# Decoder layer on eight cores: normalised token tiles transposed by DMA instead of TensorE, reciprocal roots by GpSimd's power

## The chip, the cores and the metric

One Trainium2 chip, its 8 cores, one batch element (2048 tokens) on each; nothing is exchanged between cores. The metric is the device time of the slowest core in microseconds, as the median of repeated runs.

## What is computed

```python
h = rmsnorm(x, g_mix_norm)                      # x: (2048, 1024) f32 per core
q|k|v|glu_in|gate_in = h @ w_in + b_in          # 512|128|128|1024|2048 columns
y_attn = sliding_window_attention(q, k, v, sinks) @ w_attn_proj   # window 128, 8 query and 2 key heads
z = a * sigmoid(b)                              # GLU of glu_in, 512 channels
y_conv = silu(layernorm(causal_depthwise_conv31(z))) @ w_conv_proj + b
x = x + (sigmoid(g_attn) * y_attn + sigmoid(g_conv) * y_conv) @ w_out
x = x + (silu(h2 @ w_gate) * (h2 @ w_up)) @ w_down,  h2 = rmsnorm(x, g_ffn_norm), inner width 2816
out = rmsnorm(x, g_final)
```

## The kernel before

Tokens lie in 16 tiles of 128 (`NTT`) and 4 groups of 512 (`NTG`). Matmuls take bf16 operands and contract over the partitions, so a projection needs the normalised tokens transposed: `hT` holds them as 8 blocks of 128 features by 2048 tokens. A tile gets there in four steps: `rms_sq` (ACT, sum of squares), `rms_rstd` (ACT, 1/sqrt as Ln and then Exp with scale -0.5), `rms_apply` (DVE, times root and gain, bf16, into one of four buffers `xn`), and `rms_T`: eight 128x128 transposes on PE into one PSUM bank (line 703, or 688 for the first four tiles) and a copy from there to `hT` by DVE or ACT.

The program has three stages.

- Mixer, the loop over groups: key, value and query products, attention in four blocks (`att_scores`, a mask by affine_select on POOL at line 793, `att_pv`, `att_T`), then per group four `glu_unit`s, whose output goes through a scratch tensor in device memory (`fill_zs`: one write and four shifted reads, in SP's queue). The depthwise conv of a group (`conv_unit`, line 863) and its LayerNorm (`ln_stats`, `ln_norm`, `ln_silu`) run during the next group. In `ln_stats` the variance's root is Ln and Exp on ACT over 128x512 (`stB`), and `ln_norm` multiplies by it on POOL. The tiles of group g+1 are normalised and transposed in group g. The stage ends with the conv of group 3.
- Merge and out: `merge_unit` for 8 column blocks by 4 groups, then `out_tile` for 16 tiles (16 matmuls each, the residual added by DVE), each followed by the second RMSNorm and `rms_T`. In program text tile t is transposed after the product of tile t+3 (`rms_T(tt - 3, "act")`); the last three are transposed inside the FFN, before its third group of tokens (`late_T`).
- FFN: in four passes over the 22 inner blocks, up products over the 4 groups of tokens, down products over the 16 tiles; the last pass has the final norm and the stores.

The order on each engine is not that of the text. A list scheduler (`Sched.schedule`) goes through all recorded operations with a cost for each (`ecost` for DVE and POOL, `DMA_RATE` in bytes per us and `DMA_LAT` for transfers), takes on every engine what can start first, and among those within a small slack the earliest in the text. It also deals out the PSUM banks: four for single tiles in the mixer (`ONE`), all eight from the merges of column block 2 on (`ANY`). So an altered cost or a removed operation moves others. Each engine then runs its list in order and waits on semaphores; that holds for the DMA issues in SP's and POOL's queues as well. Line 513 is every plain matmul, 517 every activation, 527, 533, 535 and 539 are the tensor-tensor and tensor-scalar helpers, 506 the DMA helper.

Of the kernel before, what the change touches and what calls it, by code (L numbers as in the profile page):

```python
# [11 lines left out]
ALU = mybir.AluOpType  # L12
# [5 lines left out]
NTG = 4  # L18
# [38 lines left out]
DMA_LAT = 2.0  # L57
DMA_RATE = 250e3
SLACK = {"pe": 0.05, "act": 0.25, "dve": 0.25, "pool": 0.3, "sp": 0.3}
# [9 lines left out]
class Sched:  # L69
# [80 lines left out]
    def schedule(self):  # L150
# [76 lines left out]
        while left:  # L227
# [28 lines left out]
            for op in blocks[k]:  # L256
                t += op.cost
                if op.dma:
                    q = e == "pool"
                    dma_free[q] = max(t, dma_free[q]) + op.nbytes / DMA_RATE  # L260
                    op.end = dma_free[q] + DMA_LAT
                else:
                    op.end = t
                order[e].append(op.gidx)
                for i in tiles_of.get(op, ()):
                    todo[i] -= 1
# [83 lines left out]
def record(plan):  # L350
# [49 lines left out]
    EPSB = region(32)  # L400
    EM = region(64)
    WCOL = region(16 * 8 * 4)
    DEN = region(16 * 4)
# [21 lines left out]
    rstd = A.f32(RSTDO, 48)  # L425
    epsb = A.f32(EPSB, 1)
    emask = A.bf16(EM, 32)
    wcol = A.f32(WCOL, 128).rearrange("p (g m) -> p g m", g=16)
# [93 lines left out]
    def ecost(eng, n, f=1.0):  # L522
        a, b = RATE[eng]
        return a + b * n * f
# [17 lines left out]
    def cp_(eng, out, in_, r, w):  # L542
        return S.add(eng, lambda e: e.tensor_copy(out=out, in_=in_), r, w, cost=ecost(eng, nfree(out)))

# [79 lines left out]
    op("pool", lambda e: e.memset(ss, 0.0), w=["ss"])  # L624
    op("pool", lambda e: e.memset(epsb, EPS), w=["epsb"])
    op("pool", lambda e: e.memset(onesf, 1.0), w=["onesf"])
    act(rstd[:, 0:1], epsb, AF.Ln, r=["epsb"], w=["warm"])
    op("pool", lambda e: e.iota(iota_i, [[1, 128]], base=0, channel_multiplier=-1), w=["iota"])
# [40 lines left out]
    def rms_rstd(c0, n):  # L669
        cs = ["ss%d" % c for c in range(c0, c0 + n)]  # L670
        rs = ["rstd%d" % c for c in range(c0, c0 + n)]
        act(rstd[:, c0:c0 + n], ss[:, c0:c0 + n], AF.Ln, r=cs + ["epsb", "warm"], w=rs, bias=epsb)
        act(rstd[:, c0:c0 + n], rstd[:, c0:c0 + n], AF.Exp, r=rs, w=rs, scale=-0.5)

# [6 lines left out]
    def rms_T(tt, copy_eng):  # L681
        b = tt % 4
        if copy_eng == "both":
# [15 lines left out]
            return  # L699
        bank = next_bank()  # L700
        S.begin()
        for c in range(8):
            op("pe", lambda e, c=c: e.transpose(out=ps_bf[bank.banks[0]][:, c * 128:(c + 1) * 128],  # L703
                                                in_=xn[:, b, c * 128:(c + 1) * 128], identity=ident),
               r=["xn%d" % b, "ident"], w=[bank], cost=0.075)
        S.end()
        src = ps_bf[bank.banks[0]].rearrange("p (c j) -> p c j", c=8)
        dst = hT[:, :, tt * 128:(tt + 1) * 128]
        if copy_eng == "act":
            act(dst, src, AF.Copy, r=[bank], w=["hT.%d" % tt])  # L710
        else:
            cp_(copy_eng, dst, src, r=[bank], w=["hT.%d" % tt])

# [159 lines left out]
    def ln_stats():  # L873
        bm = next_bank()
        S.begin()
        for c in range(4):
            mm(ps[bm.banks[0]], ones_bf, ybf[:, c, :], c == 0, c == 3, r=["ones", "ybf.%d" % c], w=[bm])
        S.end()
        bq = next_bank()
        S.begin()  # L880
        for c in range(4):
            mm(ps[bq.banks[0]], ones_bf, ysq[:, c, :], c == 0, c == 3, r=["ones", "ysq.%d" % c], w=[bq])
        S.end()
        act(stA, ps[bm.banks[0]], AF.Square, r=[bm], w=["stA"])
        tt_("dve", stB, ps[bq.banks[0]], stA, ALU.subtract, r=[bq, "stA"], w=["stB"])
        act(stB, stB, AF.Ln, r=["stB", "epsb"], w=["stB"], bias=epsb)
        act(stB, stB, AF.Exp, r=["stB"], w=["stB"], scale=-0.5)
        tt_("dve", stA, ps[bm.banks[0]], stB, ALU.mult, r=[bm, "stB"], w=["stA"])
# [39 lines left out]
    for tg in range(NTG):  # L928
# [40 lines left out]
        for u in range(4):  # L969
            glu_unit(tg, u)  # L970
            fill_zs(tg, u)
            if nxt < NTG:
                norm_apply(nxt, u)
                rms_T(4 * nxt + u, "dve")
            if prev >= 0:
# [102 lines left out]
    for tt in range(NTT):  # L1078
        out_tile(tt)
        if tt >= 1:  # L1080
            rms_apply(x2[tt - 1], tt - 1, 1, "x.%d" % (tt - 1))
        if tt >= 3:
            rms_T(tt - 3, "act")
    rms_apply(x2[NTT - 1], NTT - 1, 1, "x.%d" % (NTT - 1))

# [19 lines left out]
    S.alias(["wd0"], ["w_out0", "w_out1"])  # L1105
    late_T = [NTT - 3, NTT - 2, NTT - 1]
    f0 = 0
    si_ = 0
    for gi, nf in enumerate(FF_GROUPS):
# [4 lines left out]
        for fi in range(nf):  # L1114
            rg = w_next()
            ru = w_next()
            for tg in range(NTG):
                if late_T and tg == 2:
                    for tt in late_T:
                        rms_T(tt, "act")  # L1120
                    late_T = []
                    S.alias(["actT.%d.%d" % (f_, t_) for f_ in (4, 5) for t_ in range(NTG)],
                            ["xn%d" % i for i in range(4)])
                bg = proj_fm(tg, lambda k: ring[rg][:, k, :], ["ring%d.0" % rg, "ring%d.1" % rg])
# [76 lines left out]
```

How the kernel before makes its waits and increments, by code:

```python
            def body(eng):  # L302
                known = {}
                for op in self.ops[ename]:
                    waits = {}
                    for d in op.deps:
                        if d.dma:
                            key, val = ("d", d.eng, d.dsem), d.dticket
                        else:
                            key, val = ("c", d.eng), d.ticket
                        if known.get(key, 0) >= val:
                            continue
                        if waits.get(key, 0) < val:
                            waits[key] = val
                    for key, val in waits.items():
                        sem = csem[key[1]] if key[0] == "c" else dsem[key[1]][key[2]]
                        eng.wait_ge(sem, val)
                        known[key] = val
                    ins = op.fn(eng)
                    if ins is None:
                        continue
                    if op.dma:
                        ins.then_inc(dsem[ename][op.dsem], 16)
                    elif op.signal:
                        ins.then_inc(csem[ename], 1)
```

## Time and profile before

| | us |
|---|---|
| median of 3 runs (lowest, highest) | 922.11 (921.85, 923.03) |
| profiled execution | 923.55 |
| its span, first to last instruction, slowest core | 922.0 |
| spans of the eight cores | 912.3 to 922.0 |
| TensorE busy | 864.5 (94%) |
| VectorE, ScalarE, GpSimd busy | 401.1, 302.2, 211.7 |

The profile is of the slowest core. Busy shares count the time in which an engine executes an instruction; waits, register work and DMA issues are left out. Where TensorE is busy nearly always, the other engines matter by what they make it wait for.

### The profile page before, as it was taken

To read this page: it belongs to the slowest core of one execution; us is meant where nothing else is said; L and a number is where in the kernel's file an instruction comes from. 1 tells how busy PE (TensorE), PEld (TensorE's weight loads), DVE (VectorE), ACT (ScalarE), POOL (GpSimd) and SP (SyncE) were. 2 spreads that over 40 slices of the span, in tenths; PEclk is the share of its full clock that TensorE was granted. 3 is DMA by queue.
4 is the path that set the end of the run, shared out by engine and by line. 5 is a ranking of instruction groups with operands and counts; after the bars stand their busy time and mean duration, and the time that the engine had idled before them with its cause. 6 is when DMAs were issued, how large, how long until landed. Compare 5 with 4: busy or idle time off the path is not lost.

```text
span 922.0 us, 14159 instructions; the slowest of 8 cores (912.3 to 922.0 us)
## 1 busy us (share of the span) xinstructions
PE 864.5 (94%) x4837; PEld 405.0 (44%) x4923; DVE 401.1 (44%) x594; ACT 302.2 (33%) x490; POOL 211.7 (23%) x232
## 2 busy tenths in 40 slices
PE   4888798985999999999999999999999999999996
PEld 2344344432444444445544444444444444444442
DVE  3265677463554343456622263114512135212286
ACT  4183866463422222256631101110011100111186
POOL 3540717373542222210001101010001100000044
PEclk9898999999999999999999999999999999999998
DMA  9965222759975333390094404442064400000035
GB/s 178 150 152 176 66 78 66 100 91 140 189 117 54 35 35 35 35 226 15 13 148 47 37 10 71 44 46 24 3 89 46 39 8 1 1 1 1 1 160 206
DMA packets 102823, 67.64 MB, mean 73 GB/s; under 512 B 73875, under 2 KB 93505, under 8 KB 102753
## 3 DMA queue, kind: packets, MB, share of 16 engines
q0 software_dynamic: 83088, 29.37, 29.9%
q1 hardware_dynamic: 19248, 37.20, 13.5%
q8 instruction: 41, 0.67, 0.3%
q14 instruction: 29, 0.24, 0.1%
q10 hardware_dynamic: 417, 0.16, 0.1%
HBM read 85.56 MB, written 10.52 MB: 104 GB/s over the span
## 4 chain that ended last, share of the span: by engine, by line
PE 86%; DMA 8%; DVE 2%; ACT 2%; issue 2%; POOL 1%; SPq 0%; POOLq 0%; DVEq 0%; ACTq 0%
PE ps L513 82%; DMA arena<-w_in 4%; PE ps L863 2%; DMA z_scratch<-arena 2%; DMA arena<-z_scratch 1%; PE ps L703 1%; ACT arena L517 1%; DMA arena<-x 1%; POOL arena L506 1%; DVE arena L539 1%; ACT L517 0%; DVE arena L527 0%; PE ps L827 0%; SPq L506 0%; DVE arena L535 0%
## 5 line engine op out<-in xcount | busy, mean ns | idle before, releaser
L513 PE MATMUL ps<-arena 128*128 128x512 bf16 (+4 forms) x3940 | 811.2, 365 | 23.3 <-DMA arena<-w_in 7.0
L513 PEld LDWEIGHTS ps<-arena 128*128 128x128 bf16 (+1 forms) x4026 | 369.9, 99 | 454.2 <-issue 46.1
L527 DVE TENSOR_TENSOR arena<-arena,ps 128x512 f32<-128x512 f32 (+1 forms) x216 | 148.5, 687 | 292.3 <-PE ps L513 290.4
L517 ACT ACTIVATE arena<-ps 128x512 f32<-128x512 f32 (+3 forms) x159 | 113.3, 722 | 385.8 <-PE ps L513 363.1
L517 ACT ACTIVATE arena<-ps,arena 128x512 f32<-128x512 f32 (+1 forms) x112 | 75.4, 686 | 151.1 <-PE ps L513 107.8
L527 POOL TENSOR_TENSOR arena<-arena 128x512 f32<-128x512 f32 (+1 forms) x64 | 74.5, 1172 | 171.6 <-ACT arena L517 169.0
L517 ACT ACTIVATE arena<-arena 128x1 f32<-128x1 f32 (+3 forms) x152 | 91.6, 617 | 52.2 <-DVE arena L535 11.1
L539 DVE SCALAR_TENSOR_TENSOR arena<-ps,arena 128x512 f32<-128x512 f32 (+1 forms) x80 | 57.9, 725 | 95.7 <-PE ps L513 79.0
L506 POOL DMA_DIRECT2D arena<-w_ffn_in x44 | 38.7, 880 | 199.2 <-PE ps L513 199.2
L539 DVE SCALAR_TENSOR_TENSOR arena<-arena 128x1024 bf16<-128x1024 f32 (+2 forms) x64 | 68.1, 1064 | 14.4 <-ACT arena L517 12.5
L793 POOL TENSOR_SCALAR_AFFINE_SELECT arena<-arena 128x1024 bf16<-128x1024 bf16 x31 | 34.9, 1124 | 74.5 <-ACT arena L517 72.4
L863 PE MATMUL ps<-arena 128*32 128x512 bf16 x512 | 34.1, 415 | 11.5 <-DMA arena<-z_scratch 11.1
L535 POOL TENSOR_SCALAR arena<-arena 128x512 f32<-128x512 f32 x32 | 20.6, 644 | 88.0 <-ACT arena L517 87.8
L517 ACT ACT_TABLE_LOAD x19 | 24.4, 1283 | 26.0 <-PE ps L513 17.7
L527 DVE TENSOR_TENSOR arena<-ps,arena 128x512 bf16<-128x512 f32 (+2 forms) x44 | 21.8, 497 | 24.9 <-PE ps L513 15.2
L506 POOL DMA_DIRECT2D arena<-w_ffn_down x4 | 3.4, 842 | 126.1 <-PE ps L513 67.2
L539 DVE SCALAR_TENSOR_TENSOR arena<-arena,ps 128x512 f32<-128x512 f32 x32 | 21.8, 685 | 14.1 <-ACT arena L517 8.4
L863 PEld LDWEIGHTS ps<-arena 128*32 128x32 bf16 x512 | 13.9, 102 | 27.2 <-issue 18.0
L527 DVE TENSOR_TENSOR arena<-arena 128x512 bf16<-128x512 f32 (+1 forms) x35 | 22.7, 649 | 5.9 <-POOL arena L533 2.4
L506 POOL DMA_DIRECT2D arena<-w_in x23 | 20.8, 922 | 16.5 <-PE ps L513 10.7
L533 DVE TENSOR_SCALAR arena<-ps,arena 128x512 bf16<-128x512 f32 x20 | 14.9, 747 | 16.4 <-PE ps L513 14.4
L533 DVE TENSOR_SCALAR arena<-arena 128x512 f32<-128x512 f32 (+2 forms) x18 | 13.2, 736 | 19.7 <-ACT arena L517 19.6
(34 smaller groups left out, 126.0 us busy)
## 6 DMA issues: line engine op xcount, KB each, us to landing
arena<-x SPq DMA_DIRECT2D x32, 512.0 KB, 6.4
arena<-w_ffn_in POOLq DMA_DIRECT2D x44, 256.0 KB, 5.4
arena<-z_scratch SPq DMA_DIRECT2D x64, 135.0 KB, 3.1
out<-arena SPq DMA_DIRECT2D x16, 512.0 KB, 2.7
arena<-w_in POOLq DMA_DIRECT2D x16, 256.0 KB, 6.4
arena<-w_in POOLq DMA_DIRECT2D x7, 512.0 KB, 21.0
arena<-w_ffn_down POOLq DMA_DIRECT2D x2, 1536.0 KB, 13.1
arena<-w_ffn_down POOLq DMA_DIRECT2D x2, 1280.0 KB, 18.0
```

The lines of the kernel that those rows point to most:

```text
L506: return S.add(eng, lambda e: e.dma_start(out=out, in_=in_, **kw), r=r, w=w, dma=True, cost=0.95 if eng == "pool" else 0.45, nbytes=nb)
L513: return S.add("pe", lambda e: e.matmul(out=out, lhsT=lhsT, rhs=rhs, start=start, stop=stop, **kw), r, w, cost=max(0.06, nfree(rhs) * 0.00 ...
L517: return S.add("act", lambda e: e.activation(out=out, in_=in_, func=func, **kw), r, w, cost=0.22 + 0.00089 * nfree(in_))
L527: return S.add(eng, lambda e: e.tensor_tensor(out=out, in0=in0, in1=in1, op=alu), r, w, cost=ecost(eng, nfree(out)))
L533: return S.add(eng, lambda e: e.tensor_scalar(out=out, in0=in0, scalar1=s1, scalar2=None, op0=op0), r, w, cost=c)
L535: return S.add(eng, lambda e: e.tensor_scalar(out=out, in0=in0, scalar1=s1, scalar2=s2, op0=op0, op1=op1), r, w, cost=c)
L539: return S.add(eng, lambda e: e.scalar_tensor_tensor(out=out, in0=in0, scalar=scalar, in1=in1, op0=op0, op1=op1), r, w, cost=ecost(eng, nf ...
L703: op("pe", lambda e, c=c: e.transpose(out=ps_bf[bank.banks[0]][:, c * 128:(c + 1) * 128], in_=xn[:, b, c * 128:(c + 1) * 128], identity=id ...
L793: op("pool", lambda e, sl=sl, pat=pat, base=base, cm=cm: e.affine_select(out=sl, in_=sl, pattern=pat, base=base, channel_multiplier=cm, co ...
L863: op("pe", lambda e, m=m, cg=cg: e.matmul(out=ps[bank.banks[0]][32 * cg:32 * (cg + 1), :], lhsT=wS[:, 4 * c + cg, m, :], rhs=zs[c][:, cg, ...
```

## The change

The transposition of all tiles but the first four becomes one DMA each, from `xn` to `hT`, in SP's queue. The RMS roots and the LayerNorm root become an addition and a power of -0.5 on POOL (for LayerNorm the addition of eps goes into DVE's subtraction). The second norm's `rms_apply` and `rms_T` stand right behind their tile in the text, and there is no `late_T`. The scheduler's costs for copies and for transfer rates differ too.

```diff
-DMA_RATE = 250e3
+DMA_RATE = (370e3, 300e3)
...
+    mhalf = A.f32(MH, 8)
...
     def cp_(eng, out, in_, r, w):
-        return S.add(eng, lambda e: e.tensor_copy(out=out, in_=in_), r, w, cost=ecost(eng, nfree(out)))
+        return S.add(eng, lambda e: e.tensor_copy(out=out, in_=in_), r, w, cost=ecost(eng, nfree(out), 0.5 if eng == "dve" else 0.4))
...
+    op("pool", lambda e: e.memset(mhalf, -0.5), w=["mhalf"])
...
-    act(rstd[:, 0:1], epsb, AF.Ln, r=["epsb"], w=["warm"])
+    act(rstd[:, 0:1], epsb, AF.Exp, r=["epsb"], w=["rstd0"])
...
     def rms_rstd(c0, n):
         cs = ["ss%d" % c for c in range(c0, c0 + n)]
         rs = ["rstd%d" % c for c in range(c0, c0 + n)]
-        act(rstd[:, c0:c0 + n], ss[:, c0:c0 + n], AF.Ln, r=cs + ["epsb", "warm"], w=rs, bias=epsb)
-        act(rstd[:, c0:c0 + n], rstd[:, c0:c0 + n], AF.Exp, r=rs, w=rs, scale=-0.5)
+        ts_("pool", rstd[:, c0:c0 + n], ss[:, c0:c0 + n], EPS, None, ALU.add, None, r=cs, w=rs)
+        tt_("pool", rstd[:, c0:c0 + n], rstd[:, c0:c0 + n], mhalf[:, 0:n], ALU.pow, r=rs + ["mhalf"], w=rs)
...
-        bank = next_bank()
-        S.begin()
-        for c in range(8):
-            op("pe", lambda e, c=c: e.transpose(out=ps_bf[bank.banks[0]][:, c * 128:(c + 1) * 128],
-                                                in_=xn[:, b, c * 128:(c + 1) * 128], identity=ident),
-               r=["xn%d" % b, "ident"], w=[bank], cost=0.075)
-        S.end()
...
+        S.add("sp", lambda e: e.dma_start(out=hT[:, :, tt * 128:(tt + 1) * 128], in_=xn[:, b, :], transpose=True),
+              ["xn%d" % b], ["hT.%d" % tt], dma=True, cost=0.6, nbytes=262144)
...
-        tt_("dve", stB, ps[bq.banks[0]], stA, ALU.subtract, r=[bq, "stA"], w=["stB"])
-        act(stB, stB, AF.Ln, r=["stB", "epsb"], w=["stB"], bias=epsb)
-        act(stB, stB, AF.Exp, r=["stB"], w=["stB"], scale=-0.5)
+        stt_("dve", stB, ps[bq.banks[0]], EPS, stA, ALU.add, ALU.subtract, r=[bq, "stA"], w=["stB"])
+        tt_("pool", stB, stB, mhalf[:, 0:1].broadcast_to([128, 512]), ALU.pow, r=["stB", "mhalf"], w=["stB"])
...
     for tt in range(NTT):
         out_tile(tt)
-        if tt >= 1:
-            rms_apply(x2[tt - 1], tt - 1, 1, "x.%d" % (tt - 1))
-        if tt >= 3:
-            rms_T(tt - 3, "act")
-    rms_apply(x2[NTT - 1], NTT - 1, 1, "x.%d" % (NTT - 1))
+        rms_apply(x2[tt], tt, 1, "x.%d" % tt)
+        rms_T(tt, "dma")
```

The line numbers move: line 513 of before is 515 of the change, 527 is 529, 793 is 785, 827 is 819, 863 is 855, 506 is 508; the transposing DMA is line 703 of the change.

The order on PE at the end of the mixer. L863 (L855) are the conv's matmuls, 32 to a unit; between them stand merge products. Before:

```order
L827 MATMUL ps<-arena 128x128 x4
L863 MATMUL ps<-arena 32x512 x32
L513 MATMUL ps<-arena 128x512 x12
L863 MATMUL ps<-arena 32x512 x32
L513 MATMUL ps<-arena 128x512 x20
L863 MATMUL ps<-arena 32x512 x32
L513 MATMUL ps<-arena 128x512 x808
```

With the change:

```order
L819 MATMUL ps<-arena 128x128 x4
L855 MATMUL ps<-arena 32x512 x64
L515 MATMUL ps<-arena 128x512 x8
L855 MATMUL ps<-arena 32x512 x32
L515 MATMUL ps<-arena 128x512 x12
L855 MATMUL ps<-arena 32x512 x32
L515 MATMUL ps<-arena 128x512 x3124
```

The first two conv units now stand together, 8 and 12 matmuls lie between the next ones, and behind the last everything is one run without a transpose.

The order in SP's queue in group 0 with the change, from the transposition of tile 4 to that of tile 7 (z_scratch is the scratch tensor, x the tokens of later tiles); before, the same queue had only the scratch and x rows:

```order
L703 DMA_TRANSPOSE arena<-arena 128x8x128
L508 DMA z_scratch<-arena 128x512
L508 DMA arena<-x 128x1024
L508 DMA arena<-z_scratch 32x4x540 x4
L703 DMA_TRANSPOSE arena<-arena 128x8x128
L508 DMA arena<-z_scratch 32x4x540 x4
L508 DMA arena<-x 128x1024
L508 DMA z_scratch<-arena 128x512
L703 DMA_TRANSPOSE arena<-arena 128x8x128
```

Each transposition takes its turn behind scratch reads, which themselves wait for the scratch write before them.

The order in POOL's queue with the change around the first LayerNorm (L785 is the attention's mask; the third row, which waits for DVE alone, is the power, and the 128x512 rows behind it are the norm's products):

```order
L529 TENSOR_TENSOR arena<-arena 128x4 [waits c_pool]
L785 AFFINE_SELECT arena<-arena 128x1024 [waits c_act] x2
L529 TENSOR_TENSOR arena<-arena 128x512 [waits c_dve]
L785 AFFINE_SELECT arena<-arena 128x1024 [waits c_act]
L529 TENSOR_TENSOR arena<-arena 128x512 [waits c_pool]
L529 TENSOR_TENSOR arena<-arena 128x512 [waits c_dve,c_pool]
L785 AFFINE_SELECT arena<-arena 128x1024 [waits c_act]
L529 TENSOR_TENSOR arena<-arena 128x512
```

The power stands between two masks, and the masks behind it wait their turn in the same queue.

## Rows read from the trace of the kernel before

**Rows 1.** The page: busy time of the engines
```profile
PE 864.5 (94%) x4837; PEld 405.0 (44%) x4923; DVE 401.1 (44%) x594; ACT 302.2 (33%) x490; POOL 211.7 (23%) x232
```

**Rows 2.** Windows: start:end, us, busy time per engine, PE clock, DMA share, GB/s
```profile
0.00:60.00 60.00, 41.27 (x280) 21.56 (x285) 22.00 (x38) 26.53 (x47) 26.92 (x44) 0.94 0.87 155
60.00:250.00 190.00, 163.38 (x1456) 79.13 (x1474) 111.14 (x169) 105.41 (x151) 89.64 (x80) 0.96 0.60 116
...
880.00:922.00 42.00, 32.98 (x151) 14.86 (x152) 30.20 (x57) 29.92 (x60) 19.56 (x16) 0.94 0.50 201
```

**Rows 3.** Waits of PE from 60 to 250 us: us in total, times, longest
```profile
PE ps L863 <- DMA arena<-z_scratch: 11.1, 3, 4.3
PE ps L827 <- DVE arena L527: 5.9, 5, 2.3
PE ps L513 <- ACT arena L517: 5.4, 5, 1.7
```

**Rows 4.** Groups by shape: count | busy us, mean ns | idle before, releasers
```profile
L703 PE MATMUL ps<-arena 128*128 128x128 bf16 x224 | 16.8, 219 | 0.5 <-DVE arena L539 0.4
...
L517 ACT ACTIVATE arena<-ps 128x1024 bf16<-128x1024 bf16 x16 | 16.2, 1024 | 15.3 <-PE ps L703 15.3
```

**Rows 5.** Timeline of PE in the out stage: start us, us, what
```profile
408.55 0.61 PE L703 MATMUL ps<-arena 128*128 128x128 bf16 x8
...
409.00 3.62 PE L513 MATMUL ps<-arena 128*128 128x512 bf16 x16
...
412.45 0.61 PE L703 MATMUL ps<-arena 128*128 128x128 bf16 x8
```

**Rows 6.** Groups from 60 to 250 us; timeline behind the last LayerNorm root
```profile
L517 ACT ACT_TABLE_LOAD x12 | 15.4, 1283 | 2.8 <-DVE arena L527 2.0 <-PE ps L513 0.5
...
241.66 5.32 POOL L527 TENSOR_TENSOR arena<-arena 128x512 f32<-128x512 f32 x4 [4.00 <-ACT arena L517]
```

**Rows 7.** POOL's 128x512 product by shape, and its timeline in group 1
```profile
L527 POOL TENSOR_TENSOR arena<-arena 128x512 f32<-128x512 f32 x48 | 64.8, 1357 | 170.1 <-ACT arena L517 169.0
...
102.89 1.43 POOL L527 TENSOR_TENSOR arena<-arena 128x512 f32<-128x512 f32 x1
...
104.27 1.09 POOL L793 TENSOR_SCALAR_AFFINE_SELECT arena<-arena 128x1024 bf16<-128x1024 bf16 x1
```

**Rows 8.** Timeline of the start, POOL and PE
```profile
8.05 6.38 POOL L506 DMA_DIRECT2D arena<-w_in  x7 [4.54 <-DMA arena<-x]
...
20.76 3.57 PE L513 MATMUL ps<-arena 128*128 128x128 bf16 x32 [2.99 <-DMA arena<-w_in]
...
32.39 12.60 PE L513 MATMUL ps<-arena 128*128 128x512 bf16 x49 [4.00 <-DMA arena<-w_in]
```

**Rows 9.** The page: DMA queues (packets, MB, share); issues, KB each, us to landing
```profile
q0 software_dynamic: 83088, 29.37, 29.9%
q1 hardware_dynamic: 19248, 37.20, 13.5%
...
arena<-x SPq DMA_DIRECT2D x32, 512.0 KB, 6.4
...
arena<-z_scratch SPq DMA_DIRECT2D x64, 135.0 KB, 3.1
```

**Rows 10.** Timeline of PE around the last transposition of group 1's tiles
```profile
68.38 0.61 PE L703 MATMUL ps<-arena 128*128 128x128 bf16 x8 [0.43 <-DVE arena L539]
...
76.06 11.00 PE L513 MATMUL ps<-arena 128*128 128x512 bf16 x70 [0.22 <-issue]
```

**Rows 11.** Timeline of PE: the last two conv units
```profile
217.87 3.29 PE L863 MATMUL ps<-arena 128*32 128x512 bf16 x32 [4.11 <-DMA arena<-z_scratch]
...
229.86 2.60 PE L863 MATMUL ps<-arena 128*32 128x512 bf16 x32 [4.29 <-DMA arena<-z_scratch]
```

**Rows 12.** Issue of nine x loads; DMA busy tenths, 404 to 426 us, 0.55 us each
```profile
395.03 6.67 SPq L506 DMA_DIRECT2D arena<-x  x9
...
DMA  9999989999999999999999200000100000000000
```

More of the change, by code:

```diff
@@ L259, in schedule @@
                     q = e == "pool"
-                    dma_free[q] = max(t, dma_free[q]) + op.nbytes / DMA_RATE
+                    dma_free[q] = max(t, dma_free[q]) + op.nbytes / DMA_RATE[q]
                     op.end = dma_free[q] + DMA_LAT
@@ L401, in record @@
     EM = region(64)
+    MH = region(32)
     WCOL = region(16 * 8 * 4)
@@ L699, in rms_T @@
             return
-        bank = next_bank()
-        S.begin()
-        for c in range(8):
-            op("pe", lambda e, c=c: e.transpose(out=ps_bf[bank.banks[0]][:, c * 128:(c + 1) * 128],
-                                                in_=xn[:, b, c * 128:(c + 1) * 128], identity=ident),
-               r=["xn%d" % b, "ident"], w=[bank], cost=0.075)
-        S.end()
[L707 to L712, printed above, removed]
+        S.add("sp", lambda e: e.dma_start(out=hT[:, :, tt * 128:(tt + 1) * 128], in_=xn[:, b, :], transpose=True),
+              ["xn%d" % b], ["hT.%d" % tt], dma=True, cost=0.6, nbytes=262144)
     def proj_fm(tg, lhs, wres):
@@ L973, in record @@
                 norm_apply(nxt, u)
-                rms_T(4 * nxt + u, "dve")
+                rms_T(4 * nxt + u, "dma")
             if prev >= 0:
@@ L1105, in record @@
     S.alias(["wd0"], ["w_out0", "w_out1"])
-    late_T = [NTT - 3, NTT - 2, NTT - 1]
+    S.alias(["actT.%d.%d" % (f_, t_) for f_ in (4, 5) for t_ in range(NTG)], ["xn%d" % i for i in range(4)])
     f0 = 0
@@ L1117, in record @@
             for tg in range(NTG):
[L1118 to L1123, printed above, removed]
                 bg = proj_fm(tg, lambda k: ring[rg][:, k, :], ["ring%d.0" % rg, "ring%d.1" % rg])
```

## The prediction

> **What bounds the kernel now.** Start with the page's busy line [rows 1]: TensorE (PE) is busy 864.5 of 922.0 us. The windows view says where the other 57.5 us lie [rows 2]: 18.7 us in the first 60, 26.6 between 60 and 250, 9.0 in the last 42, which leaves 3.2 in the 630 us between. So from 250 to 880 a microsecond of PE work removed is a microsecond gained, as long as nothing new makes PE wait; between 60 and 250 a removal may be swallowed by a wait. Which waits those are, the waits view for that stretch tells [rows 3]: 11.1 us for conv inputs read back from the scratch tensor, 5.9 for VectorE (DVE), 5.4 for ScalarE (ACT), none of note for GpSimd (POOL). The end (last norm, stores) is untouched by the change.
>
> **The change, part by part.** Durations are of one profiled execution (923.55 us), 1.4 us above the median of the runs, 922.1. I take the differences from its trace and apply them to the median.
>
> *1. PE transposes go*: 28 blocks of 8, busy 16.8 us in all [rows 4]. Neighbours overlap, so I price a block by the cadence. In the out stage (L513 is the W_out product, L703 the transpose) a block starts at 408.55, the matmuls behind it at 409.00, the next block at 412.45 [rows 5]: 3.45 us for 16 matmuls, 0.216 each, and 0.45 for the block. 16 blocks of the second norm and 12 of the mixer, 28 x 0.45 = **-12.6 us**.
>
> *2. Copies and table loads go*: 12 copies on DVE, 16 on ACT (16.2 us) [rows 4], and the table loads that switch between Ln and the attention's functions, most of the 12 (15.4 us) that lie between 60 and 250 [rows 6]. None is on the path by itself; what it can return is PE's 11.3 us of waits for ACT and DVE there [rows 3]. Bounds: nothing (the chain of scores, exp, mask, product stays as it is) and about half, 6. I take **-3 us**.
>
> *3. The LayerNorm root moves to POOL.* Four times, a power over 128x512 replaces Ln and Exp, for which POOL now waits: it is idle 4.00 us before the norm's products [rows 6]. No row has a power on POOL. Nearest below: the same instruction with a multiplication, 1.36 us (mean of 48) [rows 7]. Above: if the power is a logarithm and an exponential by polynomials, ten such passes, 13.6 us, an estimate from the same row. POOL's queue is tight there: from 102.89 on a norm product (1.43) and a mask (1.09) follow each other without a gap, and attention's products need the masks [rows 7]. About 4 us of power fit, the idle time that it replaces; beyond that each microsecond goes to PE, at four places. I take the lower end, the row of the same instruction: **0**. The upper end costs 4 x (13.6 - 4) = 38.
>
> *4. The RMS roots move to POOL*: 23 pairs, addition and power, of 128x1 or 128x4. No row has them; two products of 128x512, 2.7 us, are a far upper end, and I take 1 us a pair. At the start POOL first issues seven weight loads (8.05 to 14.43), so the first root comes near 15, and the four normalisations (1.3 us each) and their copies end near 22. PE starts the value product at 20.76, and soon waits 4.0 us for weights until 32.39 anyway [rows 8]: up to 2.5 us late, hidden there. **0**.
>
> *5. 28 transposing DMAs of 256 KB in SP's queue.* No row has one. By the queues' totals [rows 9] the hardware queue moved 37.20 MB in 13.5% of 922 us, 299 GB/s, 0.9 us a tile; the software queue, in smaller packets, 29.37 MB in 29.9%, 107 GB/s, 2.5 us a tile. To landing: 3.1 us for 135 KB, 6.4 for 512 KB, so 3 to 6. I take 1 us of queue, the row of the same queue, and 4 to landing. It costs at three places:
> - Group 1 (tiles 4 to 7). Tile 7 is transposed at 68.38, and the products that need it start at 76.06, behind a conv wait [rows 10]. The new order puts the value product ahead of the fourth conv unit, and SP's queue puts the last transpose behind a scratch write and its reads. Landing 72 to 76: **+2**, bounds 0 and 6. Groups 2 and 3 are transposed long before their products: 0.
> - The conv inputs. At the end of the mixer 8 and 12 matmuls stand between the last conv units instead of 12 and 20, under waits of 4.11 and 4.29 us that stay [rows 11]: 12 x 0.216 = **+2.6**. Bounds 0, and 6 if the scratch reads are late behind transposes.
> - The out stage. The nine x loads issued from 395.03 on keep the DMA engines full until about 416 [rows 12], and the first transposes lie behind them. The square of tile 4 needs the first buffer back, 3 to 6 us later than now. PE has eight banks, four tiles or 4 x 3.45 = 13.8 us, of cover; DVE, with some 2.7 us of work a tile against PE's 3.45, catches up. Then the tail: after the last W_out product come addition, square, POOL's pair, normalisation and landing, some 8 to 9 us, against three token groups of FFN, 48 x 0.216 = 10.4. Two large w_ffn_down loads are issued just then. **+1**, bounds 0 and 5.
>
> Sum: -12.6 - 3 + 2 + 2.6 + 1 = -10.0; 922.1 - 10.0 = **912.1 us**.
>
> The cadence rows give 0.45 us of PE for eight transposes [rows 5], and the queue rows 0.9 to 2.5 us for a tile by DMA [rows 9]. The Trainium skill speaks against the change: "VectorE: DVE Perf Modes", section "The three transpose paths", has 390 ns for a 128x128 block on TensorE, 1309 ns by DMA, and advises TensorE where PSUM will do. By its first figure term 1 would be an estimated 87 us; the trace contradicts that. By its second, eight blocks one after another, a tile would take an estimated 10.5 us; no run here shows it.
>
> **The rivals.**
> *A slow power* (slower than before). Place: POOL, ahead of the masks of groups 1 to 3 and of the merge's additions after the last conv. For: a power is far more arithmetic than a product, and POOL is tight there. Against: the instruction's form is that of the 1.36 us row. It decides from 4 x (P - 4) = 10, P = 6.5 us, on; at 13.6 the kernel takes 912 + 38 = 950. Chance 0.22, nearly half of it above 938.
>
> *Transposes as the bottleneck.* The out stage starts near 394.7 (408.55 less four tiles), ends 55.2 later, and tile 15 is needed 10.4 after that, at 460.3. From 416 that is 44.3 us for 16 transposes, 2.8 each. At 5 us each, twice the slow end, 80 - 44.3 = 36, less the 1 counted: 912 + 35 = 947. From 3.4 each on the gain is gone. For: SBUF to SBUF in short pieces is unlike an x load. Against: even the software queue's rate gives 2.5. Chance 0.10. (The page's second figure is this case.)
>
> *The removal is swallowed.* A power of 5 to 6 us, or landings of 6 with terms 5 at their bounds: -12.6 + 6 + 6 + 5 = +4, less part of term 2: 918 to 926. Chance 0.15.
>
> *Term 2 at its bound and nothing added*: 922.1 - 12.6 - 6 = 903.5, inside the forecast's own range.
>
> **How the numbers follow.** Forecast 0.53 (own range 903 to 917), slow power 0.22, slow transposes 0.10, swallowed 0.15. Below 903 I leave 0.05 and above 938 0.15: the range is 903 to 938. 0.2% is about 1.8 us, roughly what a measurement of this kernel can tell from no change. Faster by more than that: 0.53, 0.02 of the slow power (its mild end) and 0.06 of swallowed, 0.61. Within it 0.07. Slower: 0.19 + 0.09 + 0.04 = 0.32.
>
> **What would show it.** Out stage: no L703, 3.45 us a tile, PE at 9 throughout. POOL: four instructions that stand out of the 128x512 group; their duration is term 3, and PE waits for masks would be the slow power. Issue table: transposes at about 4 us to landing; PE waits that name them, over 3 us in all, say that term 5 is short. PE waits on the scratch tensor near 14 us, on ACT and DVE near 8. If those grow while the two new operations are as cheap as I take them, the order of the work did it, and my reasons are wrong even where the time fits.

## The result, and the profile after

The changed kernel takes 1.3577 times as long as before, 95% interval 1.3547 to 1.3606: 1251.9 us against 922.1. All times below are such ratios times 922.1 us, with their intervals; runs in which one die ran at a lower clock are left out of them. Where an expectation quotes the median of a run's own times (941.9, 923.1, 907.5), it can differ from that by 2 us.

The page of the changed kernel: busy time (share of the span, number of instructions), and the span in 40 slices of 31.3 us, each digit the busy share in tenths.

```profile
PE 860.5 (69%) x4618; PEld 393.9 (31%) x4699; DVE 394.0 (31%) x582; ACT 251.3 (20%) x404; POOL 562.3 (45%) x283
...
PE   4773019302910261039999997599999999999997
...
POOL 4518995999699959993222222010011011000024
PEclk9997559755965686559999999799999999999999
```

TensorE's busy time has hardly moved [rows 1]; what is new is that it stands still. Four holes lie in the first 560 us, and in each POOL is at 9. A fifth, short one comes near slices 25 and 26, where POOL is at 2 and 0. The waits of TensorE name both causes.

```profile
PE ps L515 <- DVE arena L529: 310.9, 4, 78.7
PE ps L515 <- DMA arena<-arena: 21.2, 1, 21.2
PE ps L855 <- DMA arena<-z_scratch: 16.2, 4, 9.6
```

The first row names VectorE (L529), and VectorE is not at fault. One of the four, in the timelines of POOL, DVE and PE (start, duration, and in brackets the idle time before and who ended it):

```profile
100.34 81.93 POOL L529 TENSOR_TENSOR arena<-arena 128x512 f32<-128x512 f32 x1 [0.22 <-DVE arena L541]
182.24 1.09 POOL L785 TENSOR_SCALAR_AFFINE_SELECT arena<-arena 128x1024 bf16<-128x1024 bf16 x1
...
182.38 0.69 DVE L529 TENSOR_TENSOR arena<-ps,arena 128x512 f32<-128x512 f32 x1 [79.97 <-POOL arena L529]
...
183.21 10.41 PE L515 MATMUL ps<-arena 128*128 128x512 bf16 x61 [77.80 <-DVE arena L529]
```

The power takes 81.93 us. The mask behind it on POOL waits, as the prediction feared. VectorE waits too: its product of mean and root is the next in its queue, and 79.97 us long nothing else leaves that queue, no eviction either. TensorE, in need of a bank, resumes right behind that product. The chain of waits holds all four powers and, at the end of the out stage, one more item:

```profile
100.34 81.94 POOL arena L529
223.62 81.94 POOL arena L529
344.70 81.96 POOL arena L529
470.40 81.96 POOL arena L529
...
777.07 18.79 DMA arena<-arena
```

The last transpose is issued at 777.07 and lands 18.79 us later. Between 765 and 800 us the DMA view shows what it shares the engines with (packets, MB, share; then the issues, with the median us to landing):

```profile
q0 software_dynamic: 1312, 2.62, 49.7%
...
arena<-w_ffn_down POOLq DMA_DIRECT2D x2, 1280.0 KB, 17.0
arena<-g_final SPq DMA_DIRECT2D x1, 512.0 KB, 15.9
arena<-arena SPq DMA_TRANSPOSE x4, 11.3
```

And the groups of POOL by shape, all of whose L529 rows with f32 in and out but the first are powers alone (the first holds 48 norm products and four powers):

```profile
L529 POOL TENSOR_TENSOR arena<-arena 128x512 f32<-128x512 f32 x52 | 391.9, 7540 | 169.3 <-ACT arena L519 163.3 <-DVE arena L541 3.9 <-POOL arena L529 0.4
L529 POOL TENSOR_TENSOR arena<-arena 128x1 f32<-128x1 f32 x20 | 11.3, 566 | 3.0
...
L535 POOL TENSOR_SCALAR arena<-arena 128x1 f32<-128x1 f32 x20 | 7.4, 372 | 44.2 <-ACT arena L519 44.2
L529 POOL TENSOR_TENSOR arena<-arena 128x4 f32<-128x4 f32 x3 | 3.1, 1040 | 0.4
```

The bill from profile to profile is 1252.4 - 922.0 = 330.4 us of span. Power waits give 310.9, the last transposes 21.2, scratch waits 16.2 - 11.1 [rows 3] = 5.1, together 337.2. TensorE's busy time fell by 4.0, and not by the 12.6 of its transposes, because its clock was granted at half in and after the holes (mean 0.858 against 0.986): 8.6 us given back. (Both traces lack some matmul records, 4837 of 4923 and 4618 of 4699, which takes about as much from either sum.) That makes 333.2; the other waits are 2.8 shorter.

### The profile page after: what moved, and what is told of

Read it like the earlier page. It is cut to its first block, busy times and chain, and to the rows that moved or that the text cites. A ratio compares the mean times of both kernels' runs of the same rounds, so it can differ in the third digit from the quotient of the medians.

```text
span 1252.4 us, 13791 instructions; the slowest of 8 cores (1239.5 to 1252.4 us)
## 1 busy us (share of the span) xinstructions
PE 860.5 (69%) x4618; PEld 393.9 (31%) x4699; DVE 394.0 (31%) x582; ACT 251.3 (20%) x404; POOL 562.3 (45%) x283
## 4 chain that ended last, share of the span: by engine, by line
PE 59%; POOL 28%; DMA 8%; issue 2%; DVE 2%; ACT 1%; SPq 1%; POOLq 0%; DVEq 0%; ACTq 0%
PE ps L515 58%; POOL arena L529 27%; DMA arena<-w_in 3%; DMA arena<-arena 2%; PE ps L855 2%; DMA arena<-z_scratch 1%; ACT arena L519 1%; DMA z_scratch<-arena 1%; DMA arena<-x 1%; DVE arena L529 1%; SPq L508 1%; POOL arena L508 0%; DVE arena L541 0%; POOL arena L785 0%; DVE arena L535 0%
## 5 line engine op out<-in xcount | busy, mean ns | idle before, releaser
L515 PE MATMUL ps<-arena 128*128 128x512 bf16 (+3 forms) x3945 | 820.0, 368 | 350.7 <-DVE arena L529 310.9
L529 POOL TENSOR_TENSOR arena<-arena 128x512 f32<-128x512 f32 (+3 forms) x91 | 416.0, 4575 | 174.7 <-ACT arena L519 163.3
L529 DVE TENSOR_TENSOR arena<-arena,ps 128x512 f32<-128x512 f32 (+1 forms) x216 | 148.2, 687 | 306.4 <-PE ps L515 305.5
L519 ACT ACTIVATE arena<-ps 128x512 f32<-128x512 f32 (+2 forms) x143 | 97.3, 688 | 393.4 <-PE ps L515 380.8
L519 ACT ACTIVATE arena<-arena 128x1024 bf16<-128x1024 f32 (+2 forms) x98 | 75.7, 788 | 448.2 <-DVE arena L537 343.2
L529 DVE TENSOR_TENSOR arena<-ps,arena 128x512 bf16<-128x512 f32 (+2 forms) x40 | 19.1, 477 | 329.0 <-POOL arena L529 320.1
L541 DVE SCALAR_TENSOR_TENSOR arena<-arena 128x1024 bf16<-128x1024 f32 (+2 forms) x64 | 67.8, 1062 | 31.2 <-POOL arena L529 24.8
L785 POOL TENSOR_SCALAR_AFFINE_SELECT arena<-arena 128x1024 bf16<-128x1024 bf16 x31 | 36.2, 1167 | 49.6 <-ACT arena L519 49.5
L537 POOL TENSOR_SCALAR arena<-arena 128x512 f32<-128x512 f32 x32 | 20.2, 632 | 82.2 <-ACT arena L519 81.9
L855 PE MATMUL ps<-arena 128*32 128x512 bf16 x512 | 33.0, 408 | 16.4 <-DMA arena<-z_scratch 16.2
L535 POOL TENSOR_SCALAR arena<-arena 128x1 f32<-128x1 f32 (+3 forms) x25 | 9.0, 362 | 60.3 <-ACT arena L519 60.1
L508 POOL DMA_DIRECT2D arena<-w_in x23 | 21.1, 932 | 9.9 <-PE ps L515 5.0
L529 DVE TENSOR_TENSOR arena<-arena 128x512 bf16<-128x512 f32 (+1 forms) x35 | 22.7, 648 | 6.0 <-POOL arena L535 2.4
L545 DVE CAST arena<-arena 128x512 bf16<-128x512 f32 (+1 forms) x17 | 8.0, 471 | 52.1 <-ACT arena L519 42.2
L855 PEld LDWEIGHTS ps<-arena 128*32 128x32 bf16 x512 | 14.1, 102 | 32.2 <-issue 22.9
L537 DVE TENSOR_SCALAR arena<-arena 128x512 f32<-128x512 f32 x16 | 18.3, 1143 | 8.8 <-POOL arena L529 8.4
## 6 DMA issues: line engine op xcount, KB each, us to landing
arena<-w_ffn_down POOLq DMA_DIRECT2D x2, 1536.0 KB, 11.7
```

Of the source, the lines that this page charges most:

```text
L508: return S.add(eng, lambda e: e.dma_start(out=out, in_=in_, **kw), r=r, w=w, dma=True, cost=0.95 if eng == "pool" else 0.45, nbytes=nb)
L515: return S.add("pe", lambda e: e.matmul(out=out, lhsT=lhsT, rhs=rhs, start=start, stop=stop, **kw), r, w, cost=max(0.06, nfree(rhs) * 0.00 ...
L519: return S.add("act", lambda e: e.activation(out=out, in_=in_, func=func, **kw), r, w, cost=0.22 + 0.00089 * nfree(in_))
L529: return S.add(eng, lambda e: e.tensor_tensor(out=out, in0=in0, in1=in1, op=alu), r, w, cost=ecost(eng, nfree(out)))
L535: return S.add(eng, lambda e: e.tensor_scalar(out=out, in0=in0, scalar1=s1, scalar2=None, op0=op0), r, w, cost=c)
L537: return S.add(eng, lambda e: e.tensor_scalar(out=out, in0=in0, scalar1=s1, scalar2=s2, op0=op0, op1=op1), r, w, cost=c)
```

## The experiments

*One part of the change alone.* On the kernel before:

```diff
-        tt_("dve", stB, ps[bq.banks[0]], stA, ALU.subtract, ...)
-        act(stB, stB, AF.Ln, ...)
-        act(stB, stB, AF.Exp, ...)
+        stt_("dve", stB, ps[bq.banks[0]], EPS, stA, ALU.add, ALU.subtract, ...)
+        tt_("pool", stB, stB, mhalf[:, 0:1].broadcast_to([128, 512]), ALU.pow, ...)
```

> The kernel before, with the LayerNorm root alone taken by GpSimd's power; this asks how much of the changed kernel's 330 us is this one instruction. Theory (the power takes 81.7 us a time and VectorE's next product waits in its queue for it, so that nothing behind moves): 4 x (81.7 - 4) = 311 us more, some 1233 us, and four TensorE waits for VectorE of about 78 us. Rival (the planner, which sees a power at the price of a product, or SP's queue with the transposes in it, makes the stalls longer than the power is): clearly less, under 1200 us.

Measured: 1239.6 us (1.3443, interval 1.3423 to 1.3463), 317.5 us more than before. The waits of TensorE:

```profile
PE ps L515 <- POOL arena L796: 240.6, 4, 80.6
PE ps L515 <- DVE arena L529: 78.7, 1, 78.7
PE ps L866 <- DMA arena<-z_scratch: 10.6, 3, 5.9
```

One instruction, four times, is nearly the whole excess. The sum of the two rows, 319.3, is near the expected 311; which engine they name is not as expected. In this order of the work TensorE asks first for a mask (L796) that stands behind the power on POOL. The cause is one, the name depends on which consumer comes first.

*The changed kernel with that part taken out.* The power becomes a product, and the LayerNorm root is left out:

```diff
-        tt_("pool", stB, stB, mhalf[:, 0:1].broadcast_to([128, 512]), ALU.pow, ...)
+        tt_("pool", stB, stB, mhalf[:, 0:1].broadcast_to([128, 512]), ALU.mult, ...)
```

> The changed kernel with a product in the power's place; the LayerNorm root is left out. This is the kernel that my forecast priced at 912 us. Theory (the power is all of the excess but for the last four transposes, which land 21 us late beside the w_ffn_down loads): 912 + 20 = 932, range 926 to 938, with one TensorE wait of 15 to 21 us for transposes and waits for VectorE back at a few us. Rival (transposes and the new order cost more elsewhere, hidden so far under the four stalls): over 940. Second rival (the late transposes were an effect of the stalls before them): 910 to 918.

Measured: 930.5 us (1.0091, 1.0078 to 1.0105). So the power is worth 1251.9 - 930.5 = 321.4 us. Waits are 310.9 of it. TensorE's busy time adds 4.6 (860.5 against 855.9), but the trace of this run has all 4699 matmul records and that of the changed kernel lacks 81. From 600 to 700 us, where TensorE never stops, the latter shows 99.53 us of busy time with nine records missing, so the 81 hide an estimated 4.2 us. Slow matmuls are then an estimated 8.8, and under 2 us is not assigned. Even with the price that the forecast used, this kernel is 8.4 us slower than before, and a wait of 20.2 us for the last transposes stayed:

```profile
PE ps L515 <- DMA arena<-arena: 20.2, 1, 20.2
PE ps L855 <- DMA arena<-z_scratch: 18.2, 4, 10.3
PE ps L515 <- ACT arena L519: 5.5, 1, 5.5
```

That the transposes were late only as an effect of the holes is thereby excluded.

*The root back on ScalarE*, the rest of the change kept (the edit is that of the first experiment, the other way round).

> The changed kernel with the LayerNorm root back on ScalarE as Ln and Exp; RMS roots stay on GpSimd and the transposes on DMA. Theory: as the run with a product, plus the table loads around four pairs (8 or 9 of 1.28 us) and ScalarE's two passes, of which I take 0 to 5 us to the path: 930 to 940, slower than before by about 1%. Rival (GpSimd's queue was as tight as I read it, so taking the root off it gives time back): at or under the run with a product.

Measured: 939.8 us (1.0192, 1.0177 to 1.0206), at the upper end of the expected: 9.3 us above the run with a product, of which the row of ScalarE's waits shows 6.2 (11.7 against 5.5). This is the base for the next two.

*Does w_ffn_down delay the last transposes?* The first edit moved the loads in the program:

```diff
-            if fi == 0:
+            if fi == (2 if gi < 2 else 0):
                 dma("pool", wd_sb[wb][:, 0:nf, :], ...
```

> As the run before it (LayerNorm root on ScalarE), with the w_ffn_down loads of FFN groups 0 and 1 issued two feature blocks later. Theory (the last transposes are slow since they share the DMA engines with 2.5 MB of w_ffn_down loads): the 15 to 21 us wait shrinks to 0 to 3 us and the kernel takes 912 to 922. Rival (the transposes of the tail are late by themselves, through SP's queue or the x loads): within 3 us of the run without this edit. The edit itself can cost only if the loads come late for the down product: a TensorE wait naming them would show it.

Measured: 940.0 us (1.0194, 1.0174 to 1.0214), no difference, and the wait stayed at 21.1. That would have spoken for the rival, had the loads moved. The timeline of POOL showed that they hadn't: the planner, which places a load where its operands allow it, issued them at 460.31 us, against 461.38 in the run before. An edit of the text is no edit of the order. So the next one gave the loads a reason to wait:

```diff
+                    r=["hT.%d" % t for t in range(12, 16)] if gi < 2 else [],
                     w=["wd%d" % wb])
...
-            dma("sp", gbc, g_fin_d.broadcast_to([128, D]), w=["gbc.0", "gbc.1"])
+            dma("sp", gbc, g_fin_d.broadcast_to([128, D]),
+                r=["hT.%d" % t for t in range(12, 16)], w=["gbc.0", "gbc.1"])
```

> As the run with the root on ScalarE, but the first two w_ffn_down loads and the g_final load are now made to wait until transposes 12 to 15 have landed; the edit before this one left these loads where they were (issued at 460.31, against 461.38), so it tested nothing. Theory (contention on the DMA engines): the last transpose is issued near 464.5 and lands 3 to 5 us later, TensorE waits about 5 us in place of 20, and the kernel takes 922 to 929. Rival (a transpose at the tail is slow without those loads): within 3 us of 941.9.

Measured: 922.8 us (1.0007, 0.9992 to 1.0021), 17.0 us less than without the edit. The chain of waits of this kernel, at the same place as above:

```profile
461.52 3.09 DMA arena<-arena
464.61 0.24 issue
464.85 10.27 PE ps L515 x40
```

and TensorE's wait:

```profile
PE ps L515 <- DMA arena<-arena: 4.5, 1, 4.5
```

The same transpose lands in 3.09 us once the loads (two of w_ffn_down and that of g_final) are out of its way, against 17.78 in the run without the edit and 18.79 in the changed kernel. That the loads delay it is shown; they were held together, so this run doesn't divide the blame between them. TensorE has no wait that names the held loads.

*The other parts alone, on the kernel before.* First the RMS roots on POOL:

```diff
-        act(rstd[:, c0:c0 + n], ss[:, c0:c0 + n], AF.Ln, ...)
-        act(rstd[:, c0:c0 + n], rstd[:, c0:c0 + n], AF.Exp, ...)
+        ts_("pool", rstd[:, c0:c0 + n], ss[:, c0:c0 + n], EPS, None, ALU.add, None, ...)
+        tt_("pool", rstd[:, c0:c0 + n], rstd[:, c0:c0 + n], mhalf[:, 0:n], ALU.pow, ...)
```

> The kernel before with the 23 RMS roots alone on GpSimd (addition and power of 128x1 or 128x4, 0.22 to 0.95 and 0.57 us each). Theory (hidden, as forecast): 920 to 924, no difference. Rival (at the start the roots stand behind GpSimd's weight loads and delay everything): 2 to 4 us slower, to be seen in TensorE's idle time of the first 60 us, 18.7 before.

Measured: 920.1 us (0.9978, 0.9962 to 0.9993), a gain of 2.0, between 0.6 and 3.5 by the interval. The table loads went from 19 to 11:

```profile
L519 ACT ACT_TABLE_LOAD x11 | 14.1, 1283 | 16.4 <-PE ps L515 8.2 <-issue 5.9 <-DVE arena L529 2.0
```

Then the transposes that aren't needed soon: tiles 0 to 12 of the second norm, and with the next run tiles 8 to 15 of the mixer too. The others stay on TensorE, and no cost of the planner is changed. The last line of the diff belongs to the second of the two runs.

```diff
     def rms_T(tt, copy_eng):
         b = tt % 4
+        if copy_eng == "dma":
+            S.add("sp", lambda e: e.dma_start(out=hT[:, :, ...], in_=xn[:, b, :], transpose=True), ...)
+            return
...
-            rms_T(tt - 3, "act")
+            rms_T(tt - 3, "dma")
...
-                rms_T(4 * nxt + u, "dve")
+                rms_T(4 * nxt + u, "dma" if nxt > 1 else "dve")
```

> The kernel before, with only the transposes of tiles 0 to 12 of the second norm on DMA; the last three stay on TensorE, late, as they are; all roots stay on ScalarE. Theory (each transpose off TensorE is 0.45 us of path, as long as it isn't needed soon): 13 x 0.45 = 5.9 us less, 915 to 918, faster than both. Rival (transposes behind the x loads, or a DMA in the out stage that holds back a buffer of the normalised tile, stall the stage): 922 or more.

> As the run before, with the transposes of the mixer's groups 2 and 3 (tiles 8 to 15) on DMA as well; group 1 stays on TensorE. Theory (they are wanted a whole group later, and nothing else is in a hurry): 8 x 0.45 = 3.6 us less again, 911 to 915. Rival (in SP's queue they delay the scratch writes and reads of the conv inputs): TensorE's waits on the scratch tensor grow from 11 us by 3 to 6, and the time is that of the run before or above it, 916 to 920.

Measured: 915.1 us (0.9924, 0.9895 to 0.9953) and 911.9 us (0.9889, 0.9861 to 0.9917): 7.0 us for 13 transposes, 10.2 for 21, so 0.54 and 0.49 us each, against the 0.45 taken from [rows 5]. The intervals leave about 2.7 us either way, so the two prices are no finer than 0.33 to 0.75 and 0.36 to 0.61. Scratch waits stayed near before's 11.1 (10.3 and 12.2). In the window of the out stage TensorE never stops; the row is start:end, its length, and busy PE, PEld, DVE, ACT, POOL, then clock, DMA share, GB/s, of the second run:

```profile
400.00:465.00 65.00, 65.00 (x321) 30.21 (x319) 38.10 (x46) 29.24 (x64) 3.48 (x4) 1.00 0.80 143
```

The DMA engines are at 0.80 there, and 13 transposes behind nine x loads held nothing up.

*The price by the column.* The changed kernel, with the power over half the columns (the root of the other 256 is left out):

```diff
-        tt_("pool", stB, stB, mhalf[:, 0:1].broadcast_to([128, 512]), ALU.pow, ...)
+        tt_("pool", stB[:, 0:256], stB[:, 0:256], mhalf[:, 0:1].broadcast_to([128, 256]), ALU.pow, ...)
```

> The changed kernel with the power over 256 of the 512 columns; the root of the other 256 is left out. Theory (a power costs by the column, 0.157 us each from the 128x1 and 128x4 rows, 0.57 and 1.04 us, plus 0.41): 40.6 us an instruction in place of 81, four TensorE waits 41 us shorter each, so 1252 - 164 = 1088, range 1078 to 1098. Rival (a fixed part dominates, or the stall is longer than the power): clearly above 1100.

Measured: 1093.5 us (1.1859, 1.1837 to 1.1880), and

```profile
L529 POOL TENSOR_TENSOR arena<-arena 128x256 f32<-128x256 f32 x4 | 164.6, 41140 | 4.0 <-DVE arena L541 4.0
L529 POOL TENSOR_TENSOR arena<-arena 128x512 f32<-128x512 f32 x48 | 63.9, 1338 | 165.1 <-ACT arena L519 163.3 <-POOL arena L529 0.4
```

41.14 us for 256 columns, 81.94 for 512: 0.159 us a column and 0.3 fixed. The 128x1 and 128x4 rows above give nearly the same law: 0.157 us a column and 0.41 fixed. The product beside it takes 1.34 us, a sixty-first of the power.

*Together, and what is left.* The kernel before with 21 transposes on DMA and the RMS roots on POOL (the edits of the run with the RMS roots alone and of the run with 21 transposes), and the same with group 1 too (`"dma"` for every `nxt`):

> The kernel before with 21 transposes on DMA (tiles 8 to 15 of the mixer, 0 to 12 of the second norm) and the RMS roots on GpSimd. Theory (the two gains add): 912.0 less 2.0 = 910, range 907 to 913, the fastest so far. Rival (GpSimd's root is one more hop between the square and the transposing DMA in the out stage, and takes back what it gave): 912 or more.

> As the run before, with group 1 of the mixer (tiles 4 to 7) on DMA as well. Theory (forecast's term for group 1: -1.8 for TensorE, +2 for landing late, bounds 0 and +6): 0 to +4 us against the run before, with TensorE's idle time between 60 and 100 up from 1 to 5 us to 7 to 9, as in all kernels that have it. Rival (it is free, like groups 2 and 3): 1 to 2 us faster than the run before.

Measured: 908.7 us (0.9855, 0.9841 to 0.9868), the fastest kernel of this study, 13.4 us below before and 343 below the changed kernel; and 913.5 us (0.9907, 0.9892 to 0.9922) with group 1. Those four transposes cost 4.8 us net, a little over the 0 to 4 expected, and 6.6 with the 1.8 that they should have brought. TensorE waits 2.7 us for them, in two pieces; the rest lies in an order that differs elsewhere too, so 4.8 is the price of the edit with its new order and not of a landing.

That the order matters was the next finding. On the fastest kernel, only the change's three planner costs:

```diff
-DMA_RATE = 250e3
+DMA_RATE = (370e3, 300e3)
...
-        return S.add(eng, ... e.tensor_copy(...), r, w, cost=ecost(eng, nfree(out)))
+        return S.add(eng, ... e.tensor_copy(...), r, w, cost=ecost(eng, nfree(out), 0.5 if eng == "dve" else 0.4))
```

> As the run with both parts, with the change's three new planner costs (DMA rate by queue, copies on VectorE at half and GpSimd at 0.4 of the price). Theory (what is left between 923 us, the changed kernel with its two faults out, and 910 is the group 1 transposes, the last three transposes and the order in which the out stage normalises; costs alone do little): within 2 us of that run. Rival (the costs put the conv constants and waits of the first 100 us in another order, which is where the changed kernel loses 5 to 7 us): 3 us slower or more.

Measured: 920.5 us (0.9983, 0.9974 to 0.9992), 11.8 us slower by numbers that no engine ever executes; the expectation of no more than 2 us was wrong. The windows from 40 to 100 us show where two thirds of it went, first of the fastest kernel:

```profile
40.00:100.00 60.00, 52.64 (x450) 24.98 (x449) 32.10 (x51) 38.09 (x58) 21.05 (x22) 0.97 0.69 175
...
400.00:500.00 100.00, 100.00 (x483) 46.05 (x481) 43.12 (x54) 27.53 (x46) 23.11 (x36) 1.00 0.67 102
```

and with the new costs:

```profile
40.00:100.00 60.00, 44.97 (x396) 21.09 (x394) 28.32 (x46) 32.39 (x49) 14.55 (x15) 0.89 0.65 153
...
400.00:500.00 100.00, 96.66 (x460) 44.47 (x459) 47.23 (x58) 27.63 (x46) 22.85 (x38) 0.98 0.74 122
```

TensorE idles 7.7 us more between 40 and 100 us (ahead of 40 it had won 1.4, 26.2 us busy against 24.8), and 3.3 more in the out stage. Is that a property of the costs? Four runs ask: the costs alone on the kernel before; the old costs in the changed kernel with its other two faults out; and on the fastest kernel the rate alone, and the copies alone.

> The kernel before with nothing but the three new planner costs. Theory (the new costs order the first 250 us worse, whatever the rest): 928 to 936. Rival (each edit makes the planner find another order, and the 12 us of the last run were that of one order, no property of the costs): 918 to 926, no clear difference.

> The changed kernel with the root on ScalarE and the three loads held back, as in the run that took 923.1, and with the old planner costs. Theory (the costs are what is left of the loss): 910 to 915. Rival (group 1 and the last three transposes are what is left): 919 to 924.

> As the run with both parts (907.5 us), with the new DMA rates of the planner alone. Theory (the rate, 300 and 370 GB/s for 250, makes the planner place work on loads that land later than it thinks: PE's order begins as in the 920 us run, 45 small products in one piece): 916 to 922. Rival: 906 to 911, and the copies' price is the cause.

> As the run with both parts (907.5 us), with the new price of copies alone (half on VectorE, 0.4 on GpSimd). Theory (the rate is the cause): 906 to 911. Rival (the copies are): 916 to 922. Both in between would say that neither is, but the order that the planner happens on.

| kernel | old costs | new costs |
|---|---|---|
| before | 922.1 | 921.6 (0.9995, 0.9984 to 1.0006) |
| changed, root on ScalarE, loads held | 915.6 (0.9930, 0.9914 to 0.9945) | 922.8 |
| fastest | 908.7 | 920.5 |
| fastest, new rate only | | 915.6 (0.9929, 0.9913 to 0.9945) |
| fastest, new copy prices only | | 910.3 (0.9872, 0.9850 to 0.9894) |

The same three costs make no clear difference in the kernel before (0.5 us, inside the interval), and 7.2 and 11.8 us of loss in the other two. The changed kernel with old costs, at 915.6, came out just above the 910 to 915 expected. On the kernel before, the new costs win 4.0 us of TensorE's time ahead of 40 us and lose 4.8 between there and 100:

```profile
0.00:40.00 40.00, 27.23 (x197) 14.92 (x199) 14.14 (x24) 9.89 (x23) 15.09 (x27) 1.00 1.07 179
40.00:100.00 60.00, 48.64 (x441) 24.08 (x445) 33.59 (x52) 43.75 (x63) 24.15 (x26) 0.97 0.54 144
```

against, in the kernel before,

```profile
0.00:40.00 40.00, 23.18 (x167) 13.25 (x170) 12.35 (x22) 11.75 (x25) 20.11 (x36) 0.91 1.03 160
40.00:100.00 60.00, 53.43 (x436) 25.49 (x441) 32.02 (x49) 37.30 (x56) 13.01 (x14) 0.94 0.56 153
```

The loss between 40 and 100 us recurs in all three (in the changed kernel 46.53 us busy against 52.35); whether something pays for it depends on the rest. The rate carries the larger part of the loss on the fastest kernel, 6.9 us; it was expected to carry all (916 to 922). The copy prices alone cost 1.6, no clear difference, and the two apart give 8.5 of the 11.8. Which placement of the new order makes the loss wasn't tried apart, and stays open.

## Why the prediction was wrong

It gave 912.1 us, in a range of 903 to 938, against 1251.9. It forecast faster; it is far slower, beyond its own slow rival too.

*Step 3, the LayerNorm root, failed, and in its price alone.* "About 4 us of power fit ... beyond that each microsecond goes to PE, at four places" is right: 4 x (81.94 - 4) = 312 us, measured 310.9. The rival's place, POOL's queue, holds too. Its decision point, 6.5 us, does not: it balances a gain of 10 us that this kernel doesn't have, since with a product in the power's place it takes 930.5. What failed in this step is P. I took the row of "the same instruction with a multiplication", 1.36 us, and as upper end ten passes of it, 13.6 us; it took 81.94, sixty passes. An instruction's form (engine, operands, shape) says nothing of an operation for which no row of that engine exists; "nearest row" was a poor guide, the bound above it a guess at an algorithm. The chance of 0.22 was on the right mechanism with a size six times short. The Trainium skill, "GPSIMD Engine Reference", section "4.1 Engine selection", puts two-input elementwise work on GpSimd at about twice VectorE's time, for addition, product and maximum. The product stays in that range (1.34 us, against 0.69 for VectorE's 128x512 in the timeline above); the power is outside what the rule covers, and the rows of this study give the missing price.

*What I missed beside it.* I looked for who waits for POOL: masks and merge additions. VectorE waits too, in order, with all evictions behind it. Here both waits cover the same 80 us (the mask starts at 182.24, VectorE's product at 182.38), so the omission cost the sum nothing.

*Step 4, the RMS roots,* was right: 1 us a pair taken, 0.37 + 0.57 = 0.94 measured, 1.27 for 128x4. Alone they gain 2.0 us, table loads that fall away included, so no cost of them shows on the path; how much of step 2's 3 us the loads return was not measured apart. From their two shapes alone (0.57 and 1.04 us) the price of step 3 could have been worked out, but the trace of before has neither.

*Step 1* was right within what the runs resolve: 0.45 us a transpose taken, 0.49 to 0.54 measured, with what its copies free. (The 3.2 us of idle time that the prediction reads between 250 and 880 us are missing matmul records: the run with the RMS roots alone, whose trace lacks none, is busy for all 630 us there, with 3016 matmuls against the 2956 recorded before.)

*Step 5, the queue and landing,* was right as a price and wrong at the tail. SP spends 1.24 us on a transpose in the median, though up to 9.9 (taken: 1), and it lands in 3.9 us in the median of all 28, 3.1 in that of the out stage's 16 (taken: 4, bounds 3 and 6). "Two large w_ffn_down loads are issued just then" stood in the prediction, and was priced within "+1, bounds 0 and 5"; it is 17.0 us by the runs with and without them. Two parts of the tail's sum fail. The landing is 18.79 us beside these loads. And the cover isn't 10.4 us:

```profile
771.19 0.69 DVE L541 SCALAR_TENSOR_TENSOR arena<-ps,arena 128x512 f32<-128x512 f32 x1 [0.17 <-PE ps L515]
...
699.68 75.27 PE L515 MATMUL ps<-arena 128*128 128x512 bf16 x341
796.11 2.72 PE L515 MATMUL ps<-arena 128*128 128x512 bf16 x6 [21.15 <-DMA arena<-arena]
```

The last W_out sum runs on VectorE at 771.19, and TensorE stops at 774.95, 3.8 us later, which is room for 17 of the 48 FFN matmuls. So the planner had put most of the three token groups ahead of the last W_out products. Even an undisturbed landing waits 4.5 us. Group 1 is 6.6 us where I took 2 with a bound of 6, with the reservation above. The conv inputs (+2.6) are 5.1 in the scratch waits of the changed kernel.

*The rival of transposes as the bottleneck* was wrong in its mechanism: the stage isn't held at some microseconds a tile, one landing at its end is. The Trainium skill, "VectorE: DVE Perf Modes", section "The three transpose paths", gives 1309 ns by DMA for a block, which would have eight blocks in an estimated 10.5 us; the trace has the tile landing in 3.1 us. The same page's "Rules for kernel authors" (not the section that the prediction names for it) advises TensorE where PSUM will do as destination. Where DMA engines have room and TensorE is the bound, following that costs 0.5 us a tile here. At the tail it holds: the last tile of the changed kernel takes 18.79 us beside other loads, and the fastest kernel, which leaves the last three tiles on TensorE, is busy for all of the 100 us from 400 to 500.

*The planner's costs* got no term of their own: I read the new order and summed what I saw as 2 and 2.6. It is 7.2 us in this kernel. "The order of the work did it" was the right caution, at the wrong size.

With the power's price right, the sum would have given 912 + 312 = 1224 us. For the 28 us above that, the runs offer the tail, 17 less the 1 taken, the planner's costs, 7, and the slow matmuls behind the holes, an estimated 9: 32 in all. These were measured in different kernels, and the planner's 7 contain part of the 2 and 2.6 already taken, so the account closes only roughly.

## What to carry to other kernels

Before an operation moves to an engine on which no row shows it, time it at its full size, or refuse to call its price a range; a queue in order makes each microsecond of it a microsecond for all that stands behind, on the waiting engine too. Transposes by DMA pay where the tile is wanted long after and the DMA engines have room, and cost where the first reader is near and a large load is issued in the same microseconds: hold the load by a dependence, since moving its line moves nothing under a planner. And a planner's cost table is a part of the kernel that can be worth 1%, or nothing, depending on the kernel around it; measure it apart from the edit that it comes with.

## What the runs showed of the hardware that was not expected

- GpSimd's power: 0.57 us for 128x1, 1.04 for 128x4, 41.14 for 128x256, 81.94 for 128x512, so 0.159 us a column on 0.3 to 0.4 fixed, where a product of 128x512 takes 1.34.
- A 256 KB transposing DMA takes 1.23 us of SP's queue and lands in 3.1 us where no large load is in flight; it lands in 18.79 us beside 2.6 MB of loads in the software queue and 0.5 MB in its own.
- A hole costs more than itself. Six windows of the changed kernel, three from the end of the first hole and three around the late landing (columns as above): the granted clock is 0.50, the 1.2 GHz level, at the end of both holes, and 1.00, the 2.4 GHz level, again from 190 and from 802 us on. In between TensorE works, partly at the lower level. Over the kernel that is the 8.6 us of busy time above, and the run with a product, free of the four holes, agrees (an estimated 8.8):

```profile
182.00:186.00 4.00, 2.79 (x7) 1.05 (x8) 1.98 (x3) 0.00 (x0) 3.86 (x4) 0.50 0.11 37
186.00:190.00 4.00, 3.99 (x26) 1.75 (x26) 2.92 (x3) 2.12 (x3) 4.00 (x4) 0.60 0.54 138
190.00:200.00 10.00, 9.08 (x91) 5.00 (x91) 9.13 (x15) 4.86 (x7) 9.86 (x9) 1.00 0.29 76
790.00:796.00 6.00, 0.00 (x0) 0.00 (x0) 0.00 (x0) 0.00 (x0) 0.00 (x0) 0.50 1.18 222
796.00:802.00 6.00, 5.67 (x18) 2.31 (x20) 0.19 (x1) 0.60 (x1) 0.97 (x1) 0.65 0.08 33
802.00:810.00 8.00, 8.00 (x39) 3.64 (x38) 1.87 (x3) 1.19 (x2) 0.87 (x1) 1.00 0.68 66
```
